# Attention over paged keys in a fused decoder step: the second half of the past keys turned at the head of the next turn, value pages first in SyncE's queue

## The reference, cut to what matters

```python
DEC_BATCH = 8; DEC_SEQ = 8; PAST_LEN = 512; PAGE_SIZE = 128; H_B = 16; HD_B = 64
def stick_breaking(q, k, v, bias, q_offset):
    z = jnp.einsum('bqhd,bkhd->bhqk', q, k) * (HD_B ** -0.5) + bias[None, :, None, None]
    mask = jnp.arange(Lk)[None, :] < (q_offset + jnp.arange(Lq))[:, None]
    u = jnp.where(mask, jax.nn.log_sigmoid(-z), 0.0)
    rev_excl = lax.cumsum(u, axis=3, reverse=True) - u
    A = jnp.where(mask, jnp.exp(jax.nn.log_sigmoid(z) + rev_excl), 0.0)
    return jnp.einsum('bhqk,bkhd->bqhd', A, v)
# run_trunk, layer 1
kv = rmsnorm(h, g_kv) @ w_kv                      # keys and values of the new tokens
q = rmsnorm(h, g_mix[l]) @ w_q_b[j]
o = stick_breaking_blocked(q, k_all, v_all, sb_bias[j], past_len)
h = h + o @ w_out_b[j]
h = h + sq_relu_mlp(rmsnorm(h, g_mlp[l]), w_up[l], w_down[l])
```

## Time and profile before

| | |
|---|---|
| median of 3 runs | 1513.22 us (1513.2 to 1514.81) |
| profiled execution, its own time | 1521.05 us |
| its span | 1519.3 us |
| TensorE matmul busy | 1452.0 us, 96% |
| VectorE / ScalarE / GpSimd busy | 1143.2 (75%) / 763.9 (50%) / 391.8 us (26%) |
| mean granted clock of TensorE | 0.985 of full speed |

### The profile page before, as it was taken

How to read it: one execution, slowest core, us unless ns; L and a number is a source line. 1 busy time by engine, 2 the same in 40 slices (tenths; PEclk the granted TensorE clock), 3 DMA queues, 4 the chain that set the end, 5 groups by cost and what they waited for, 6 DMA issues and landing times.

```text
span 1519.3 us, 32621 instructions
## 1 busy us (share of the span) xinstructions
PE 1452.0 (96%) x12792; PEld 1374.2 (90%) x12792; DVE 1143.2 (75%) x1847; ACT 763.9 (50%) x1168; POOL 391.8 (26%) x451
## 2 busy tenths in 40 slices
PE   8999999999999999999998788888899999999998
PEld 8999999989999999999996667776699999999998
DVE  7866666668898989889726566666678989898753
ACT  6544444426654636455513345544556546364543
POOL 3000000002322322323154433443243223232221
PEclk9999999999999999999998899999999999999999
DMA  5133333223787786877457877775247777777721
GB/s 189 57 86 87 86 86 86 86 87 93 154 171 170 167 173 147 174 167 151 120 133 232 236 219 235 237 234 164 72 105 153 162 178 157 169 161 163 170 84 63
DMA packets 247702, 222.63 MB, mean 147 GB/s; under 512 B 12364, under 2 KB 228500, under 8 KB 247572
## 3 DMA queue, kind: packets, MB, share of 16 engines
q1 hardware_dynamic: 156722, 154.69, 33.4%
q0 software_dynamic: 72768, 56.64, 22.1%
q10 hardware_dynamic: 18082, 9.48, 2.3%
HBM read 192.19 MB, written 11.80 MB: 134 GB/s over the span
## 4 chain that ended last, share of the span: by engine, by line
PE 77%; DVE 8%; DMA 4%; issue 4%; ACT 3%; SPq 3%; POOL 1%; DVEq 0%; ACTq 0%
PE acc L2821 21%; PE acc L3145 17%; PE pMO L3145 12%; PE pL L3145 12%; DMA KT<-KX 3%; PE acc L3245 3%; SPq L540 2%; PE pL L2942 1%; DVE pg L2583 1%; DVE KX L2490 1%; DMA wraw<-in_w_up_dram 1%; PE acc L3082 1%; PE acc L3337 1%; PE pMO L3011 1%; PE acc L3502 1%
## 5 line engine op out<-in xcount | busy, mean ns | idle before, releaser
L677 POOL TENSOR_TENSOR wlo<-wraw,whi 128x512 fp32r<-128x512 f32 x40 | 56.1, 1433 | 453.5 <-ACT whi L806 453.5
L2821 PE MATMUL acc<-xa_hi,whi 128*128 128x288 f32 x544 | 125.0, 311 | 0.6 <-issue 0.6
L892 ACT ACTIVATE hi<-wraw 128x1024 fp32r<-128x1024 f32 x60 | 63.7, 1062 | 112.9 <-DVE wraw L2007 112.9
L2821 PE MATMUL acc<-xa_hi,wlo 128*128 128x288 f32 x544 | 116.4, 295 | 0.0
L2821 PE MATMUL acc<-xa_lo,whi 128*128 128x288 f32 x544 | 116.1, 295 | 0.0
L3145 PE MATMUL acc<-X_hi,hi 128*128 128x288 f32 x384 | 113.4, 295 | 0.2
L3145 PE MATMUL acc<-X_lo,hi 128*128 128x288 f32 x384 | 113.3, 295 | 0.0
L875 ACT ACTIVATE hi<-wraw 128x1024 fp32r<-128x1024 f32 x60 | 63.7, 1061 | 98.6 <-PE acc L3145 98.3
L3145 PE MATMUL acc<-X_hi,lo 128*128 128x288 f32 x384 | 113.2, 295 | 0.0
L2022 DVE TENSOR_TENSOR lo<-wraw,hi 128x1024 fp32r<-128x1024 f32 x60 | 73.4, 1223 | 40.4 <-ACT hi L875 40.2
L3145 PE MATMUL acc<-H_hi,hi 128*128 128x288 f32 x336 | 99.3, 296 | 1.3 <-DVE lo L2028 1.3
(11 more groups left out here) (512 smaller groups left out, 5013.2 us busy)
## 6 DMA issues: line engine op xcount, KB each, us to landing
wraw<-in_w_up_dram SPq DMA_DIRECT2D x64, 512.0 KB, 7.0
wraw<-in_w_down_dram SPq DMA_DIRECT2D x64, 512.0 KB, 6.5
Kp<-in_cache_k_dram SPq DMA_DIRECT2D x32, 512.0 KB, 5.4
Vp<-in_cache_v_dram SPq DMA_DIRECT2D x32, 512.0 KB, 5.0
wraw<-in_w_in_a_dram SPq DMA_DIRECT2D x30, 512.0 KB, 5.0
KT<-KX POOLq DMA_DIRECT2D x144, 64.0 KB, 2.8
wraw<-in_w_up_dram POOLq DMA_DIRECT2D x32, 256.0 KB, 5.1
S_even<-in_w_up_dram POOLq DMA_DIRECT2D x32, 256.0 KB, 7.5
```

The lines of the kernel that those rows point to most:

```text
L677: ins = pool.tensor_tensor(wlo[s][:, k:k + 2, :], wraw[s][:, k:k + 2, :], whi[s][:, k:k + 2, :].bitcast(F32), ALU.subtract)
L892: act.activation(blocks4(hi31), by_depth(G % 2)[:, 0], ACT.Copy).then_inc(piece_hi, 1)
L2821: last = pe.matmul(acc[a][:, hf, 0:HALF], w[s][:, k, a * P:(a + 1) * P], x[k][:, hf * HALF:(hf + 1) * HALF], start=(k == 0 and n == 0), st ...
```

## The change

In the steady turn, VectorE transposes pages 2 and 3 of the next sequence at the head of the next turn (one ahead of the first mask, one ahead of the first product) and no longer ahead of `Oc`; pages 0 and 1 are transposed ahead of `new_out`. In the entry, pages 2 and 3 of sequence 0 are transposed behind the queries. SyncE issues the value pages at the start of a turn, and both last key pages behind the moves of the first half. TensorE does the second `past_logits` ahead of `new_values` and shifts a few fills. The output projection's first operands (`ob_high(0..3)`, `ob_low(0..2)`) are made at the end of turn 6, and its parts are spread otherwise over the last turn. The diff, without two small hunks:

```diff
@@ -567,22 +567,25 @@
 
-            def pages_and_weights(j, weights, more_pages):
-                if more_pages:
+            def pages_and_weights(j):
+                value_pages(j + 1)
+                key_store(j)
+                keys_moved(j + 1, 1)
+                if j < NPAIR - 2:
+                    kv_weights(j + 2, 1)
                     key_page(j + 2, 0)
                     key_page(j + 2, 1)
-                key_store(j)
-                keys_moved(j + 1, 1)
+                else:
+                    ob_weights(1)
                 value_store(j)
-                value_pages(j + 1)
-                if weights:
-                    weights(0)
-                if more_pages:
+                if j < NPAIR - 3:
+                    kv_weights(j + 3, 0)
+                elif j == NPAIR - 3:
+                    ob_weights(0)
+                if j < NPAIR - 2:
+                    keys_moved(j + 2, 0)
                     key_page(j + 2, 2)
-                    keys_moved(j + 2, 0)
                     key_page(j + 2, 3)
-                if weights:
-                    weights(1)
 
@@ -605,13 +608,9 @@
             key_page(1, 3)
-            for a in range(2):
-                kv_weights(2, a)
-            pages_and_weights(0, lambda a: kv_weights(3, a), True)
-            for j in range(1, NPAIR - 3):
-                pages_and_weights(j, lambda a: kv_weights(j + 3, a), True)
-            pages_and_weights(NPAIR - 3, ob_weights, True)
-            pages_and_weights(NPAIR - 2, None, False)
+            kv_weights(2, 0)
+            for j in range(NPAIR - 1):
+                pages_and_weights(j)
             sp.wait_ge(O_full, NSEQ)
@@ -1374,6 +1373,10 @@
                 act.wait_ge(AV_free, m + 1)
+                if m < 5:
+                    act.wait_ge(AV_full, NPAIR - 1)
+                else:
+                    act.wait_ge(kv_done, 2 * NPAIR)
                 act.activation(xb_hi[:, m, 0:SEQ], attn_o[:, m, 0:SEQ], ACT.Copy).then_inc(ao_hi, 1)
@@ -1475,32 +1478,30 @@
                 q_new_rows(j + 1)
+                if j == NPAIR - 2:
+                    for m in range(4):
+                        ob_high(m)
                 weights_in(1)
 
             def last_pair(j):
-                act.wait_ge(kv_done, 2 * NPAIR)
-                ob_high(0)
                 k_rows(j)
-                ob_high(1)
                 gates(j, 0)
-                ob_high(2)
                 new_gates(j)
                 v_rows(j)
-                ob_high(3)
+                ob_high(4)
                 gates(j, 1)
                 at_copy(j, 0)
                 at_copy(j, 1)
                 gates(j, 2)
                 new_copies(j)
-                ob_high(4)
                 at_copy(j, 2)
                 ob_high(5)
                 at_copy(j, 3)
                 ob_high(6)
                 at_copy(j, 4)
-                wsplit(1, U_OB // 2 + 1, U_OB // 4 + 1)
                 act.wait_ge(os_sum, 2)
                 act.activation(xb_hi[:, :, SEQ:T], attn_o[:, :, SEQ:T], ACT.Copy).then_inc(os_hi, 1)
+                wsplit(1, U_OB // 2 + 1, U_OB // 4 + 1)
                 attn_out(j)
@@ -2492,9 +2493,9 @@
             for m in range(NB):
-                if m >= NB - 2:
-                    for g in range(2):
-                        keys_turned(0, 2 * (m - NB + 2) + g)
+                if m == NB - 2:
+                    keys_turned(0, 0)
+                    keys_turned(0, 1)
                 dve.wait_ge(unit_done, U_Q + m + 1)
@@ -2619,35 +2620,43 @@
 
+            def ob_low(m):
+                dve.wait_ge(ao_hi, m + 1)
+                dve.tensor_tensor(xb_lo[:, m, 0:SEQ], attn_o[:, m, 0:SEQ], xb_hi[:, m, 0:SEQ].bitcast(F32), ALU.subtract
+                                  ).then_inc(x_ready, 1)
+
             def pair(j, first, more):
+                if not first:
+                    keys_turned(j + 1, 2)
                 mask(j, 0)
                 if not first:
                     past_store(j)
+                    keys_turned(j + 1, 3)
                 products(j, 0, 0)
                 new_rows(j)
                 new_mask(j)
                 products(j, 0, 1)
                 weights(j, 0, 0)
+                mask(j, 1)
+                weights(j, 0, 1)
+                new_products(j)
                 if first:
                     past_out_even(0)
                     past_out_odd(0)
-                mask(j, 1)
-                weights(j, 0, 1)
+                products(j, 1, 0)
+                mask(j, 2)
                 if first:
                     past_store(0)
                     keys_turned(1, 2)
                     keys_turned(1, 3)
-                new_products(j)
-                products(j, 1, 0)
-                mask(j, 2)
                 products(j, 1, 1)
                 kv_copy(j + 1, 0)
                 weights(j, 1, 0)
                 weights(j, 1, 1)
-                new_out(j)
                 if more:
                     keys_turned(j + 2, 0)
                     keys_turned(j + 2, 1)
+                new_out(j)
                 for hh in range(2):
@@ -2658,27 +2667,20 @@
                     queries(j + 2)
-                    keys_turned(j + 2, 2)
-                    keys_turned(j + 2, 3)
+                else:
+                    for m in range(3):
+                        ob_low(m)
                 past_out_even(j + 1)
                 past_out_odd(j + 1)
                 kv_copy(j + 1, 1)
 
-            def ob_low(m):
-                dve.wait_ge(ao_hi, m + 1)
-                dve.tensor_tensor(xb_lo[:, m, 0:SEQ], attn_o[:, m, 0:SEQ], xb_hi[:, m, 0:SEQ].bitcast(F32), ALU.subtract
-                                  ).then_inc(x_ready, 1)
-
             def last_pair(j):
-                ob_low(0)
                 mask(j, 0)
-                ob_low(1)
+                past_store(j)
                 products(j, 0, 0)
                 new_rows(j)
                 new_mask(j)
-                past_store(j)
                 products(j, 0, 1)
-                ob_low(2)
                 weights(j, 0, 0)
...
@@ -2720,6 +2722,8 @@
             queries(0)
+            keys_turned(0, 2)
+            keys_turned(0, 3)
             kv_copy(0, 0)
...
@@ -3388,17 +3391,17 @@
                 fill(5, 8)
+                past_logits(j + 1, 1)
                 new_values(j)
-                past_logits(j + 1, 1)
                 weights_transposed(j, 2)
                 fill(8, 9)
                 weights_transposed(j, 3)
-                fill(9, 12)
+                fill(9, 13)
                 weights_transposed(j, 4)
-                fill(12, 13)
+                fill(13, 14)
                 weighted(j)
                 past_transposed(j + 1)
-                fill(13, 15)
+                fill(14, 15)
                 past_values(j + 1)
@@ -3435,23 +3438,23 @@
                 ob_prompt_part(0, 0)
-                ob_prompt_part(1, 0)
+                ob_prompt_part(0, 1)
                 new_rows(j)
                 values_transposed(j)
-                ob_prompt_part(0, 1)
+                ob_prompt_part(0, 2)
+                logits(j, 1)
+                ob_prompt_part(1, 0)
+                ob_prompt_part(0, 3)
                 ob_prompt_part(1, 1)
-                logits(j, 1)
-                ob_prompt_part(0, 2)
-                ob_prompt_part(1, 2)
                 weights_transposed(j, 0)
                 weights_transposed(j, 1)
                 new_sums(j)
                 logits(j, 2)
-                ob_prompt_part(0, 3)
+                ob_prompt_part(1, 2)
                 ob_prompt_part(1, 3)
+                ob_prompt_part(0, 4)
                 new_values(j)
                 weights_transposed(j, 2)
-                ob_prompt_part(0, 4)
                 ob_prompt_part(1, 4)
```

More of the change, by code:

```diff
@@ L3379, in pair @@
                 logits(j, 1)
-                fill(2, 4)
+                fill(2, 5)
                 if first:
                     past_finish(0)
-                fill(4, 5)
                 weights_transposed(j, 0)
```

## The result

| | before | after |
|---|---|---|
| median, runs taken side by side | 1514.01 us (1513.2 to 1519.3, 4 runs) | 1494.17 us (1489.92 to 1496.13, 4 runs) |
| ratio of the medians | | 0.986, 95% interval 0.9832 to 0.9888 |
| profiled execution, span | 1521.05, 1519.3 us | 1492.76, 1490.9 us |
| matmul busy, clock | 1452.0 us, 0.985 | 1441.6 us, 0.990 |

The account below looks back on a forecast made before the run. It took TensorE, 96% busy, as the bound, losing time in waits for `Oc` and in the clock behind them. Savings of 5.5 + 0.9 + 36.1 + 4.5 = 47.0 us took the median from 1513.2 to 1466 us, range 1458 to 1482.

Parts of the forecast that it names:

- Steady turn: Turns with the new order: 29.4 us each, taken between 29.0 and 29.8; six turns save 36.1 us.
- the late key page: Steady turn's head: key page 2, behind the first-half moves in SyncE's queue, lands 0.85 us late.
- the rival with 0.15: Second-half moves late behind the value pages, TensorE waiting at the second `past_logits`: 1478 to 1492 us, chance 0.15.
- The limit of 29.9 us by the DMA capacity: Steady turn: 8.3 MB a turn at 277 GB/s takes 29.9 us, so the DMA engines come just to their limit.
- The rule of ring order: SyncE's second-half moves stand behind 2 MB of value pages, through at 7.6 us; issue lasts until 8.9, so no cost.
- Entry: Stage's start: the wait for `qT` goes, second-half moves land by 807.6, 5.5 us saved (bounds 3 and 6.5).
- the gaps trade: Turn 0: the wait for `dN` shrinks by 2.3 us, that for moves grows from 3.9 to 6.5; 0.9 saved.
- Turn 6: The turn before the last has no new keys and stays at 28.4 us.
- a rival with 0.10: GpSimd's issue stands among its moves, costing 5 to 7 us each time: 1471 to 1478 us, chance 0.10.
- Last turn: Turn after turn 6: TensorE ends at 27.5 us against 32.2, 4.5 us saved (bounds 1 and 6).
- Same saving for the median: Whole kernel: the saving for the profiled execution, 1521.05 to 1474 us, taken unscaled for the median, 1513.2 to 1466.
- the sum of 47.0: Total saving in us: entry 5.5, turn 0 0.9, six turns 36.1, last turn 4.5.

Follow-up runs that it names:

- e11_split6: The changed kernel with the sixteen moves of a half dealt out 6 to SyncE and 10 to GpSimd, not 7 and 9: 1493.08 us, one run.
- e12_before_again: The kernel before the change, without an edit, in one more profiled execution: 1515.97 us.
- all three repairs: The changed kernel with moves split 8 and 8, `ob_low(3)` back in turn 6, and turn 0's old VectorE order with key pages ahead of moves: 1483.16 us.

## Why the prediction came out wrong

The saving of the steady turns and the mechanism behind it came (turns 1 to 5: 27.8 us forecast, 28.7 measured). What failed are the terms of the sum at both ends of the pipeline (entry, turn 0, turn 6 and last turn, forecast 20.4 us too short together) and the step from the profiled execution to the median.

- **Steady turn**: right, in mechanism and size. 29.21 us against 29.4; the two halves of the change add (2.30 + 3.34), and the small waits lie within 0.4 us of the walk. The last tenths are luck: the late key page that the 29.4 half counted in didn't come, and `sg` was later than walked. SyncE's second-half moves, the rival with 0.15, were late only twice, by 0.90 and 1.04 us in turns 3 and 5. The limit of 29.9 us by the DMA capacity was no limit: all five turns are shorter (29.03 to 29.46), since they move 7.6 to 8.0 MB and not 8.3, and the engines reach 300 GB/s (1006.36 to 1013.00) and not 277. The rule of ring order in the Trainium skill (DMA: Bandwidth & Descriptors, Queues, rings and completion order) left the sum as it stood, and the steady turns bear that out. The rule alone doesn't explain the late moves of the entry, since GpSimd's queue was as late there.
- **Entry**, "moves landed 2.4 behind the last issue", 5.5 saved: failed, none saved. The landing took 5.3 with 1 MB of key pages ahead. Put right (1.5 us, entry 17.02), it is given back in turn 0. I had looked at the DMA capacity for the steady turn alone. Entry and turn 0 move 239 GB/s over 65.43 us, 15.6 MB: my 17.4 + 39.2 = 56.6 asked for 276 GB/s, more than any steady turn has. That this is what makes turn 0 give back the entry's gain is argued, not shown.
- **Turn 0**, "the gaps trade": 2.7 us off. The wait for moves is 5.34 and not 6.5, but I hadn't asked what is queued behind them: key pages (2, 0) and (2, 1), VectorE's 8.32 us, and `sg`. With the old order on VectorE and on SyncE turn 0 takes 40.49.
- **Turn 6**, "no new keys and stays at 28.4": right but for GpSimd's stop, which I had as a rival with 0.10, "5 to 7 us each time". It came once, at the 129th move again, and cost 5.0; without it the turn is 28.11. The mistake was to take it for chance. The row named an exact place, two moves into the 15th half, and counting gives 128; the stop stands there in all nine profiled executions with nine moves a half. The Trainium skill's cause for such a stop (SBUF — State Buffer, SBUF: two separate sides), a port that VectorE holds, would let it move with VectorE's work; here it moved with the count alone, and VectorE was idle for the last 3.2 of its 4.85 us in `e11_split6`. Why the 129th move stops stays open.
- **Last turn**, 27.5: the walk took the waits of before over and didn't follow each portion's operand. `ob_low(3)` was 3.06 late with a half clock behind it; with it in place the last turn takes 28.90, 29.66 and 28.89. The 1.4 us and more over 27.5 that are left have no cause here.
- **"Same saving for the median"**: wrong. I said that nothing tied the 7.8 us between profiled execution and median to this stage. `e12_before_again` ties 5 us of them to it. The sum closes: 28.0 us between 1466.2 and 1494.17 are 18.7 missing in the profiled execution (19.2 in the stage by the sum of 47.0, less 0.5 won outside it), 7.8 that the profiled execution of before lay above its median, and 1.4 that the profiled one of after lay below its own. This is arithmetic; two executions of the kernel before don't say how long its usual stage is.

Of the 19.4, the runs give back 5.3 (turn 6), 5.1 (last turn) and 1.4 (turn 0) with named causes; the entry's 6.1 is bound to turn 0's transfers, and what order of both would be shortest stays open. With all three repairs the median is 1483.16, still 1 us above the range.

## What to carry to other kernels

Walk the ends of a pipeline as carefully as its steady turn: the five middle turns came within 1 us together, and what was missed lies in the two places on either side, where an operand or a page is ordered once and no repetition shows it. Where a stop stands in a trace once, count the instructions of its kind up to it before calling it chance. A sum made against one profiled execution needs a second one of the same kernel, if its own time is off the median: what is long in it may be the very stage that the change repairs. And where a repair is worth less than the scatter between groups of runs, look for its turn in the rows of several executions; here five medians within 2.5 us told nothing.

## What the hardware showed that I had not expected

- GpSimd's 129th move waits 4.85 to 8.27 us for nothing that the profile names, in ten profiled executions and whatever the turn; 128 moves go without a stop in four.
- Moves of 64 KB land 1.5 us behind their last issue with nothing ahead of them and 5.3 us with two key pages of 512 KB ahead, and those in GpSimd's queue, which holds no page, are as late (5.2 each from issue to landing, against 2.2).
- The same kernel twice: behind a wait of 2.46 us TensorE stayed at full clock (2.4 GHz, 1.00 over the entry), behind one of 3.95 it fell to half (1.2 GHz, 0.85 over the entry). Behind the waits of 4.53, 4.22 and 3.06 us of the changed kernel it fell as well. But behind 3.60 us it stayed at 1.00 and behind 2.40 it fell, in one execution (`e12_before_again`): a wait's length alone doesn't tell what it costs.
